# Rounding each weight unit in two operations of half its steps in a one-core fp32 decoder step

## The reference, cut to what matters

```python
z = rmsnorm(x) @ w_in                       # 2048 x 4096: q, k, v and the state-space input u
attn = diff_attend(rope(q), rope(k), v)     # 8 heads
y = s5_scan(u); y = gelu(y); y = y * sigmoid(y @ w_glu + b_glu)
x = x + concat(attn, y) @ w_out             # 2048 x 2048
h = rmsnorm(x)
q = h @ w_q                                 # 2048 x 2048; top 16 of 128 x 128 product keys, 8 heads
act = gelu(u_tab[idx] . h)                  # 16384 experts of 2048
x = x + sum(gate * act * v_tab[idx])
y = rmsnorm(x, g_final)
```

## Time and profile before

| | before |
|---|---|
| median of 3 runs | 3651.08 us (3650.06 to 3653.28) |
| span of the profiled execution | 3652.9 us |
| PE busy | 3478.7 us, 95% of the span |
| POOL busy | 2086.9 us, 57% |
| DVE busy | 2002.7 us, 55% |
| ACT busy | 1066.8 us, 29% |
| mean share of DMA engines busy, stages E and F | 0.70 and 0.79 |

### The profile page before, as it was taken

One profiled execution on the slowest core, in us unless ns is written; L12 is line 12 of the kernel. 1 busy time (PEld: TensorE's weight loads), 2 busy tenths in 40 slices (PEclk: granted clock), 3 DMA queues, 4 the chain that ended last, 5 costly groups with the idle time before them and its releaser, 6 DMA issues. The chain is left out here.

```text
span 3652.9 us, 58356 instructions
## 1 busy us (share of the span) xinstructions
PE 3478.7 (95%) x22668; PEld 3291.4 (90%) x22668; DVE 2002.7 (55%) x3924; ACT 1066.8 (29%) x1164; POOL 2086.9 (57%) x1667
## 2 busy tenths in 40 slices
PE   6999987889989999999999999998999999999997
PEld 6988854558989999999999999998999999999997
DVE  7831223234126897864454544443666666666665
ACT  4111132343223232333333333332222222222222
POOL 2533316004443457766666666665877777777773
PEclk9999989999999999999999999999999999999998
DMA  4598878663331236777777777777877877878773
GB/s 152 193 364 314 333 286 279 216 234 119 117 123 70 81 117 231 283 272 273 302 282 271 273 289 291 275 273 268 309 291 290 299 298 292 301 282 307 296 293 136
DMA packets 257979, 910.81 MB, mean 249 GB/s; under 512 B 98401, under 2 KB 131682, under 8 KB 179426
## 3 DMA queue, kind: packets, MB, share of 16 engines
q1 hardware_dynamic: 178386, 557.38, 42.8%
q0 software_dynamic: 36864, 268.45, 17.8%
q10 hardware_dynamic: 42576, 83.07, 6.1%
HBM read 828.34 MB, written 78.12 MB: 248 GB/s over the span
## 5 line engine op out<-in xcount | busy, mean ns | idle before, releaser
L127 POOL TENSOR_TENSOR wl<-raw,wh 128x512 fp32r<-128x512 f32 x1280 | 1758.2, 1405 | 1177.7 <-ACT wh L121 1177.2
L121 ACT ACTIVATE wh<-raw 128x2048 fp32r<-128x2048 f32 x324 | 620.7, 1916 | 2057.1 <-PE acc L1854 721.9
L1852 PE MATMUL acc<-vh,wh 128*128 128x392 f32 x2048 | 703.7, 344 | 27.5 <-DVEq L1910 14.1
L1516 PE MATMUL acc<-hh,wh 128*128 128x392 f32 x2048 | 709.8, 347 | 3.7 <-POOL wl L127 3.7
L1517 PE MATMUL acc<-hl,wh 128*128 128x392 f32 x2048 | 698.5, 341 | 0.0
L1853 PE MATMUL acc<-vl,wh 128*128 128x392 f32 x2048 | 696.5, 340 | 0.0
L1518 PE MATMUL acc<-hh,wl 128*128 128x392 f32 x2048 | 696.1, 340 | 0.0
L1854 PE MATMUL acc<-vh,wl 128*128 128x392 f32 x2048 | 695.7, 340 | 0.0
L145 PE MATMUL acc<-hh,wh 128*128 128x256 f32 (+1 forms) x1920 | 547.1, 285 | 9.5 <-DVE tt L425 6.1
L146 PE MATMUL acc<-hl,wh 128*128 128x256 f32 (+1 forms) x1920 | 544.5, 284 | 0.0
L147 PE MATMUL acc<-hh,wl 128*128 128x256 f32 (+1 forms) x1920 | 542.7, 283 | 0.0
(11 more groups left out here) (338 smaller groups left out, 3644.6 us busy)
## 6 DMA issues: line engine op xcount, KB each, us to landing
raw<-units SPq DMA_DIRECT2D x324, 1024.0 KB, 4.9
kr<-cache_k SPq DMA_DIRECT2D x128, 512.0 KB, 6.6
vr<-cache_v SPq DMA_DIRECT2D x128, 512.0 KB, 5.9
expert_acts<-ast ACTq DMA_DIRECT2D x128, 196.0 KB
expert_gates<-gs ACTq DMA_DIRECT2D x14, 1792.0 KB
a<-expert_acts SPq DMA_DIRECT2D x32, 784.0 KB
g<-expert_gates SPq DMA_DIRECT2D x32, 784.0 KB
output_steps<-qo ACTq DMA_DIRECT2D x16, 288.0 KB, 7.6
```

The lines of the kernel that those rows point to most:

```text
L121: act.activation(m.wh[s][:, :, :], m.raw[s][:, :, :], ACT.Copy).then_inc(m.hi_done, 1)
L127: x = pool.tensor_tensor(m.wl[s][:, part, :], m.raw[s][:, part, :], m.wh[s][:, part, :].bitcast(F32), ALU.subtract)
L1516: pe.matmul(o, m.wh[s][:, k, :], m.hh[:, k, NA:T], start=(k == 0), stop=False)
L1852: pe.matmul(o, m.wh[s][:, 4 * e + d, :], vh[gg][:, e, :], start=(e == 0), stop=False)
```

## The change

`split_hi` makes its activation in two operations of 8 steps (1024 elements per partition) each, each raising `hi_done` by one. `split_lo` waits for the first half before its first two subtractions and for the second half before its last two. The two places where DVE takes a remainder wait for both halves.

```diff
 def split_hi(m, act, u, s, pair, used=None):
     act.wait_ge(m.raw_in[s], pair * 16 + 16)
     act.wait_ge(*(used or (m.mm_done, u + 1)))
-    act.activation(m.wh[s][:, :, :], m.raw[s][:, :, :], ACT.Copy).then_inc(m.hi_done, 1)
+    for k in range(0, KT, KT // 2):
+        act.activation(m.wh[s][:, k:k + KT // 2, :], m.raw[s][:, k:k + KT // 2, :], ACT.Copy).then_inc(m.hi_done, 1)
 
 def split_lo(m, pool, u, s):
-    pool.wait_ge(m.hi_done, u + 1)
     for k in range(0, KT, KT // 4):
+        if k % (KT // 2) == 0:
+            pool.wait_ge(m.hi_done, u * 2 + (1 + 2 * k // KT))
         part = slice(k, k + KT // 4)
         x = pool.tensor_tensor(m.wl[s][:, part, :], m.raw[s][:, part, :], m.wh[s][:, part, :].bitcast(F32), ALU.subtract)
     x.then_inc(m.lo_done, 1)
...
             def remainder(u):
-                dve.wait_ge(m.hi_done, u + 1)
+                dve.wait_ge(m.hi_done, 2 * u + 2)
...
                 for u, part in GLU_REST.get(slot, ()):
                     k = slice(4 * part, 4 * part + 4)
-                    dve.wait_ge(m.hi_done, u + 1)
+                    dve.wait_ge(m.hi_done, 2 * u + 2)
```

## The result

The changed kernel takes 3622.65 us (median of 4 runs, 3619.20 to 3624.41) beside 3652.18 us of the kernel before in the same session (4 runs, 3650.06 to 3655.02): ratio 0.9919, 95% interval 0.9905 to 0.9934. Lines from L121 on stand one or two lower in the new kernel's listing: the rounding is L122, the subtraction L129, F's matmuls L1854 to L1856, DVE's sum of products L1927, its gate product and remainder L1881 and L1885, its addition of gathered rows L1892, and E's matmuls L1518 to L1520.

A forecast was written before the change was run, and what follows sets the result against it. Bound: the chain of ACT's rounding then POOL's remainder, sometimes late for PE. Gains of 11.5 + 1.7 + 2.5 + 1.7 + 0.5 = 17.9 us take 3651.1 to 3633.2 us; range 3627 to 3643, forecast's chance 0.76.

The forecast's parts named there:

- The halves, the second half, POOL free 0.85 us earlier: ACT's rounding, every unit: a half takes 1.07 us, both 2.04, so POOL starts its subtractions 0.85 us earlier.
- 24 waits of 0.48 us in F: Stage F: 24 waits of PE for POOL's remainder, each costing 0.48 us, disappear; 11.5 us.
- Units 56 and 108, 0.85 each: Stage F, two units late behind a double gather, where POOL ends last: each gains the full 0.85 us, together 1.7.
- The DVE delay before them may shrink as its gather is issued earlier, by 0.85 each at most; I count 0: Stage F, before units 56 and 108: DVE's lateness may shrink; counted 0, with 1.7 us as the high end.
- SP's load moves forward too: SP's load, named beside POOL's gather that moves forward with `lo_done`: it moves earlier as well; no size given.
- Stage E, 2.5 us: Stage E, unit starts where PE waits for POOL: 0.85 at 1121, none kept at 1345, 0.85 at 1373, 0.80 at 1392.
- The stage ends, 1.7 us: Ends of stages D and E, where the split has no matmul beside it: 0.85 us each.
- The start, 0.5 us: Kernel start: POOL done earlier frees about one DVE addition of squares, less DVE's waits for both halves; bounds -0.3 and 0.9.
- the next wait takes the place in F: Rival, stage F: DVE's sums or the gathers hold PE instead; only 4.7 us gained, 3646 us; chance 0.11.
- POOL is slowed while ACT still rounds: Rival, every unit: the new overlap with ACT slows POOL's four subtractions by 1.55 us, giving 3673 us; chance 0.04.
- The overlap with DVE moves: Rival: POOL's earlier four meet DVE's long operations differently, half of F's gain is lost, 3640 us; chance 0.07.
- Nothing: Rival: the change does nothing because POOL is held by its gather anyway; chance 0.02.

The follow-up runs named there:

- both halves awaited: Kernel before with the rounding cut in two operations of 8 steps, POOL waiting for both before its first subtraction: 3657.41 us, ratio 1.0017.
- halves in E: Kernel before with the halves and POOL's two waits only in stage E: 3649.20 us, ratio 0.9994; once more, 3654.21 us.
- The repeats: The changed kernel, code unchanged, measured again in another session: 3624.11 us, ratio 0.9931; its first measurement gave 0.9919.

## Why the prediction was right in kind and short in size

By its own steps:

- *The halves, the second half, POOL free 0.85 us earlier*: right to 0.03 us (1.05, 2.01 and 1.14 us for 1.07, 2.04 and 1.15). The Trainium skill (Perfetto Trace Analysis, Optimizing Scalar/DVE Operations) puts one Scalar operation's access overhead at about 93 ns. By that rule, the trace agrees: two halves take 2.01 us in place of 1.92.
- *24 waits of 0.48 us in F*: right. The usual group went from 34.64 to 34.15 us, and all 24 waits are gone.
- *Units 56 and 108, 0.85 each*: right; the distances before their first matmul went from 1.24 and 1.26 to 0.41 and 0.42 us.
- *"The DVE delay before them may shrink as its gather is issued earlier, by 0.85 each at most; I count 0"*: this is the failed step in F, in its size and in its path. The delay shrank at every late place: the periods of units 54 and 106 went from 10.14 and 10.31 to 9.34 and 9.10 (0.8 and 1.2 us), and those of units 27 and 79 from 9.45 and 9.43 to 8.98 and 8.96 (0.5 each, of which 0.1 had been counted with POOL's lateness). At 54 and 106 it is not the gathered rows that DVE waits for. Timelines of SP and DVE, kernel before, then after:

```profile
2970.72 0.33 SPq L116 DMA_DIRECT2D raw<-units  x1
...
2971.93 0.38 SPq L1761 DMA_DIRECT2D g<-expert_gates  x1
...
2988.10 1.79 DVE L1879 TENSOR_TENSOR a<-a,g 128x1568 f32<-128x1568 f32 x1 [3.12 <-DMA g<-expert_gates]
```

```profile
2949.92 0.33 SPq L116 DMA_DIRECT2D raw<-units  x1
...
2951.13 0.38 SPq L1763 DMA_DIRECT2D g<-expert_gates  x1
...
2967.36 1.79 DVE L1881 TENSOR_TENSOR a<-a,g 128x1568 f32<-128x1568 f32 x1 [3.13 <-DMA g<-expert_gates]
```

  DVE's weighing waits 3.1 us for the gates, beside a pair of gathers that makes their transfer 16.2 us long instead of 11.2. Their load stands on SP behind a unit's load that waits for POOL's remainder (the load goes out 0.3 us behind POOL's end). So it is issued as much earlier as the remainder ends: 8.73 us behind the start of unit 52 before, 7.87 after, and the weighing follows (7.82 and 7.02 us behind the start of unit 54). The prediction had the step in a clause, "SP's load moves forward too", and gave it no price. At unit 106 another 0.3 us came from the transfer itself, beyond the bound of 0.85. At 27 and 79 it is POOL's four subtractions, back to back with the pair of gathers, that hold DVE's own remainder for 6.2 us; they start 0.5 us earlier. POOL and PE behind the late unit 54, kernel after (the first and the last row answer to the earlier trace rows):

```profile
2971.82 6.61 POOL L129 TENSOR_TENSOR wl<-raw,wh 128x512 fp32r<-128x512 f32 x4 [4.00 <-ACT wh L122]
...
2969.68 0.45 PE L1854 MATMUL acc<-vh,wh 128*128 128x392 f32 x1 [0.65 <-DVE xt L1927]
...
2978.56 0.44 PE L1854 MATMUL acc<-vh,wh 128*128 128x392 f32 x1
```

  In the kernel before, the row of unit 55, the one at 2969.68, had 1.32 of idle time for DVE. F gained 16.3 us in all: 11.7 and 1.7 as counted, and 3 more.
- *Stage E, 2.5 us*: the other failed step. The wait at 1121 lost its 0.84 us (3.76 to 2.92 from start to start). But the sum took idle time for the whole price of a wait. Behind the waits at 1121 and 1373 the clock fell, and 1.5 us more were lost in each next unit; both losses are gone in the changed kernel. How much of that to expect of a shorter wait the runs do not say. The wait at 1345 was to give back what it gained, by way of an exponential that waits for DVE; instead it disappeared, since POOL's four of that unit, started 0.85 us earlier against DVE's choosing, take 6.1 us instead of 7.8. Against it stands the new wait of 0.8 us before dense unit 7, whose four take 7.8. The dense units 0 to 13 gained 4.0 us instead of 1.65, the queries 2.1 instead of 0.85. How E's early part falls is not the same in every kernel with the same code: in the bad way the dense units gain 0.6.
- *The stage ends, 1.7 us*: right. The last dense unit to F went from 22.95 to 22.10, and D's last matmul to E's first transposition from 15.73 to 14.88.
- *The start, 0.5 us*: right as far as it can be told. DVE's fifteen additions of squares take 13.9 us together in all eight profiles with the start of before, the kernel with both halves awaited among them, and 13.2 to 13.5 in the five with halves. PE's matmul on their sum starts 29.3 to 31.0 us behind PE's first before and 28.4 to 28.9 with halves. What is left of it at the end of stage A, which varies by 4 us, no run tells.

So 17.9 becomes: F 16.3, E 6.1, ends 1.7, together 24.1 us that repeat in both profiles of the changed kernel. The rest up to the 29.5 us of the medians lies in A, M, F's first unit (11.4 and 10.0 us in two executions of one kernel, halves in E) and the tail, where single executions differ by more than the change can be made to show. The repeats, at 0.9931 and 0.9919, hold it at 25 to 30 us; whether the last 1 to 5 us belong to the change stays open.

Of the rivals, *the next wait takes the place in F* is dead: DVE's places in F became shorter. *POOL is slowed while ACT still rounds* is dead: 5.04 and 6.60 us as before. *The overlap with DVE moves* did happen, in E: in the changed kernel mostly in favour, which the rival, drawn as a loss only, did not allow for, and in five other profiles at a loss, some 3 us where the two ways can be compared. *Nothing* is dead.

## What to carry to other kernels

When an operation in an engine's queue ends earlier, everything queued behind it does too: price what stands behind it, and what waits for that (here SP's load of a unit, behind it the gates, behind them DVE's sums) at its likeliest shift, not at nothing. Ask at each late place which wait ends last: at two of four it was the transfer of the gates, not the gathered rows. A wait of the matmul engine of 2 us and more can cost more than its length, through the clock behind it, so read the length of the unit after a wait as well as the wait. Once a chain fits, cutting it finer gives little (0.85 to 1.3 us of shift: 2 us in F), while the order in two queues (one gather ahead of the subtractions, loads that wait for nothing ahead of one that waits) gave some 4 us of F and 6 us of the kernel.

## What was not expected of the hardware

ScalarE's rounding took 632, 1052, 1473 and 1916 ns for 512, 1024, 1536 and 2048 elements per partition: 0.82 to 0.87 ns an element and about 0.2 us an operation, of which the next one's start covers half (two halves 2.01 us). After an idle time of PE the same unit took 1.5 us more or not, behind distances of 2.16 and 2.20 us between matmuls; another took 1.4 us more behind 2.51 and nothing more behind 3.40. One and the same code in E took 115.3 or 118.6 us, by which of two engines came first at a near tie. A transfer of the gates issued with the second of two gathers took 16.1 to 16.6 us in all 37 cases, the others 12.8 at most but for one of 14.8.
